# First attention of a decoder trunk: q and k copies in a used ring slot, keys turned between two v units, probabilities scaled by a diagonal while they are turned

## The reference, cut to what matters

```python
h = rms_norm(x, norm_mix[0])
p = h @ w_in_ab                        # columns: z (512) | q (768) | k (768) | v (768)
a_out = gmlp_spatial_gating(z)         # u * (w @ rms_norm(v) + b), causal, chunks of 128
q, k = rope(rms_norm(q)), rope(rms_norm(k))        # 12 heads of 64
for g in range(3):                                 # window/dilation groups, 4 heads each
    sc = q @ k.T / 8 ; masked by causality, window and dilation of the group
    m, l, o = max(sc), sum(exp(sc - m)), exp(sc - m) @ v / l
b_out = sum over g of softmax_g(m + log l) * o     # the groups merged by their denominators
x = x + concat(a_out, b_out) @ w_out_ab
x = x + swiglu(rms_norm(x, norm_ffn[0]), ffn weights)
# layer 2: MoBA attention and a short convolution, then top-2-of-8 SwiGLU experts
```

## Time and profile before

| | us |
|---|---|
| time, median of 3 runs | 1371.06 |
| the 3 runs | 1370.25, 1371.33, 1371.06 |
| the profiled execution, its own time | 1370.74 |
| its span in the profile | 1369.0 |
| TensorE busy | 1354.6 (99%) |
| VectorE busy | 1178.0 (86%) |
| ScalarE busy | 1017.7 (74%) |
| GpSimd busy | 121.3 (9%) |

### The profile page before, as it was taken

The page is one execution under the profiler, slowest core; times in us unless marked ns, Lnnn a source line. Parts: engine busy times, 40 slices in busy tenths (PEclk is TensorE's granted clock), DMA queues, the critical chain, the costliest instruction groups (busy, mean ns, idle before and its releaser), DMA issues.

```text
span 1369.0 us, 19886 instructions
## 1 busy us (share of the span) xinstructions
PE 1354.6 (99%) x6885; PEld 1140.2 (83%) x6885; DVE 1178.0 (86%) x1371; ACT 1017.7 (74%) x1189; POOL 121.3 (9%) x130
## 2 busy tenths in 40 slices
PE   9999999999999999999999999999999999999998
PEld 7778999988888788888888888888888888888886
DVE  5876655568969999999999999999999999999998
ACT  5656444456758778888888888888888888888886
POOL 1020000000230220200200110020020002003000
PEclk9999999999999999999999999999999999999999
DMA  9944543643657999999999999999999999999980
GB/s 346 362 139 170 185 154 124 217 153 123 247 202 294 364 381 359 393 397 372 368 394 397 353 391 400 369 370 394 396 352 392 398 360 378 394 386 361 393 335 31
DMA packets 184624, 430.90 MB, mean 315 GB/s; under 512 B 6076, under 2 KB 14032, under 8 KB 184576
## 3 DMA queue, kind: packets, MB, share of 16 engines
q1 hardware_dynamic: 181136, 422.81, 83.0%
q0 software_dynamic: 3440, 7.44, 2.5%
HBM read 425.68 MB, written 7.36 MB: 316 GB/s over the span
## 4 chain that ended last, share of the span: by engine, by line
PE 90%; DVE 6%; issue 1%; DMA 1%; ACT 1%; POOL 0%; DVEq 0%; POOLq 0%; ACTq 0%
PE psum L781 29%; PE psum L783 28%; PE psum L782 28%; DVE w_lo L428 2%; PE psum L1353 2%; DVE w_lo L410 1%; DMA slot_table<-routing,table_row 1%; DMA routing<-slot_table 0%; PE psum L813 0%; PE psum L1212 0%; PE psum L914 0%; POOL slot_table L705 0%; PE psum L1222 0%; DVE probs L2107 0%; PE psum L1055 0%
## 5 line engine op out<-in xcount | busy, mean ns | idle before, releaser
L428 DVE TENSOR_TENSOR w_lo<-raw_ring,w_hi 128x1024 fp32r<-128x1024 f32 x674 | 807.1, 1222 | 48.4 <-ACT w_hi L423 11.9
L423 ACT ACTIVATE w_hi<-raw_ring 128x1024 fp32r<-128x1024 f32 x675 | 713.1, 1061 | 165.4 <-PE psum L783 164.5
L781 PE MATMUL psum<-w_hi,xg_hi 128*128 128x512 f32 x896 | 351.1, 392 | 1.0 <-DVE w_lo L428 0.9
L783 PE MATMUL psum<-w_hi,xg_lo 128*128 128x512 f32 x896 | 348.9, 389 | 0.0
L782 PE MATMUL psum<-w_lo,xg_hi 128*128 128x512 f32 x896 | 348.7, 389 | 0.0
L410 DVE TENSOR_TENSOR w_lo<-raw_ring,w_hi 128x1024 fp32r<-128x1024 f32 x124 | 151.3, 1227 | 78.0 <-ACT w_hi L402 77.1
L402 ACT ACTIVATE w_hi<-raw_ring 128x1024 fp32r<-128x1024 f32 x124 | 130.0, 1058 | 93.9 <-PE psum L783 93.6
L781 PEld LDWEIGHTS psum<-w_hi,xg_hi 128*128 128x128 f32 x896 | 168.2, 188 | 35.9 <-issue 1.9
L783 PEld LDWEIGHTS psum<-w_hi,xg_lo 128*128 128x128 f32 x896 | 168.2, 188 | 35.3
L782 PEld LDWEIGHTS psum<-w_lo,xg_hi 128*128 128x128 f32 x896 | 168.3, 188 | 34.1
L781 PE MATMUL psum<-w_hi,moe_hT_hi 128*128 128x512 f32 x448 | 175.8, 392 | 0.5 <-DVE w_lo L428 0.5
(11 more groups left out here) (299 smaller groups left out, 1340.6 us busy)
## 6 DMA issues: line engine op xcount, KB each, us to landing
raw_ring<-in_moe_w_gate SPq DMA_DIRECT2D x56, 2048.0 KB, 10.7
raw_ring<-in_moe_w_up SPq DMA_DIRECT2D x56, 2048.0 KB, 10.9
raw_ring<-in_moe_w_down SPq DMA_DIRECT2D x56, 2048.0 KB, 10.5
raw_ring<-in_ffn_w_gate SPq DMA_DIRECT2D x5, 2048.0 KB, 8.0
raw_ring<-in_ffn_w_up SPq DMA_DIRECT2D x5, 2048.0 KB, 9.1
raw_ring<-in_ffn_w_down SPq DMA_DIRECT2D x5, 2048.0 KB, 10.3
raw_ring<-in_w_in_ab SPq DMA_DIRECT2D x4, 2048.0 KB, 19.6
raw_ring<-in_w_in_cd SPq DMA_DIRECT2D x4, 2048.0 KB, 8.2
```

Of the source, the lines that this page charges most:

```text
L423: act.activation(wh[:, v % SPLITS, :], moe_raw(i, q), ACT.Copy).then_inc(hi_ready, 1)
L428: dve.tensor_tensor(wl[:, v % SPLITS, :], moe_raw(i, q), wh[:, v % SPLITS, :].bitcast(F32), ALU.subtract).then_inc(lo_ready, 1)
L781: pe.matmul(out_, sh, mh_, start=start, stop=False)
L783: return pe.matmul(out_, sl, mh_, start=False, stop=stop)
```

## The change

- `qT` and `kT` move from `R0` (on `act_hi`) to the ring slot of the fifth tile (`A_SLOT` is 4), whose last unit is 19. Copies no longer wait for the last projection unit, but for `lo_ready` 20. SyncE's load of tile 11 into that slot gets a second wait, `s_done` 8.
- TensorE turns the keys after unit 20 and before unit 21, no longer after unit 21. ScalarE now copies five groups (0 to 4), VectorE one (5). ScalarE's table load for `Exp` follows the copies. The copy of v's last columns is shared: token tile 0 by ScalarE, token tile 1 by VectorE.
- The scalings of `probs[n]` are gone from VectorE and GpSimd. VectorE writes for each item a 128x128 diagonal of the inverse sums (`diag`, identity times a column), and `turn(n)` is an ordinary float32 matrix product of a block of `probs[n]` with this diagonal in place of a transposition with the identity. For items 0 to 3 the inversion is one instruction on four columns.
- VectorE's order changes: `maximum(4)` follows `cat_ab`, `cat_T` comes before `maximum(6)`, and the inverses are spread. The waits for `s_done` 8 in `cat_T` and `out_hi` are gone.

```diff
-        qT = at("qT", [6, SEQ], F32, R0)
-        kT = at("kT", [6, SEQ], F32, R0 + 6144)
+        A_SLOT = (first["out_ab_tile"] - 2) % RING
+        qT = at("qT", [6, SEQ], F32, base + A_SLOT * TILE * 4)
+        kT = at("kT", [6, SEQ], F32, base + A_SLOT * TILE * 4 + 6144)
+        diag = at("inverse_diagonals", [8, P], F32, R0 + 4096)
...
                 if t >= RING:
                     sp.wait_ge(lo_ready, tile_last[t - RING] + 1)
+                if t == RING + A_SLOT:
+                    sp.wait_ge(s_done, 8)
...
                 def turn(n):
-                    if n in P_POOL:
-                        pe.wait_ge(p_scaled_pool, P_POOL.index(n) + 1)
-                    else:
-                        pe.wait_ge(p_scaled, P_DVE.index(n) + 1)
+                    pe.wait_ge(p_inverse, n + 1)
...
-                        mm = pe.transpose(ps[:, bk, (b % 4) * P:(b % 4 + 1) * P], probs[n][:, b * P:(b + 1) * P], ident)
+                        mm = pe.matmul(ps[:, bk, (b % 4) * P:(b % 4 + 1) * P], probs[n][:, b * P:(b + 1) * P], diag[:, n, :],
+                                       start=True, stop=True)
...
-                pe.wait_ge(qkT_act, 3)
-                pe.wait_ge(qkT_dve, 3)
+                pe.wait_ge(qkT_act, 5)
+                pe.wait_ge(qkT_dve, 1)
                 scores_pair(0)
                 pe.wait_ge(proj_act, 6)
+                pe.wait_ge(v_last, 1)
                 scores_pair(1)
...
-            project(U_V4L, first["out_ab"], 0, 5)
+            project(U_V4L, U_V4L + 1, 0, 5)
             heads_T(3, 6)
+            project(U_V4L + 1, first["out_ab"], 0, 5)
...
+                act.wait_ge(lo_ready, U_V4L)
+                for i in range(3):
+                    turned_heads(i)
                 split_hi(act, first["out_ab"] + 2)
+                turned_heads(3)
                 act.wait_ge(gv_ms, 1)
                 act.activation(small[:, HSD:HSD + 8], small[:, HMS:HMS + 8], ACT.Sqrt).then_inc(gv_std, 1)
+                turned_heads(4)
                 act.preload_act_table(ACT.Exp)
...
+                def inverse(n0, n1):
+                    c = slice(3 * n0, 3 * n1 - 2, 3)
+                    dve.wait_ge(p_ready, n1)
+                    link(dve.reciprocal(small[:, RL:RL + 24][:, c], small[:, LS:LS + 24][:, c]))
+                    for n in range(n0, n1):
+                        dve.tensor_scalar(diag[:, n, :], ident, small[:, RL + 3 * n:RL + 3 * n + 1], None,
+                                          ALU.mult).then_inc(p_inverse, 1)
```

More of the change, by code:

```diff
@@ L146, in weight_stream @@
     first["out_ab"] = len(units)
+    first["out_ab_tile"] = len(tiles)
     units += by_rows(tile(w_out_ab, 0, 4, 0, D))
@@ L508, in decoder_trunk @@
         U_GV, U_V3, U_V4L = 12, 16, 20
+        QK_AB = 5
         QUARTER_BANKS = (5, 3, 4, 1)
@@ L656, in _ @@
             rope_tables(B_MQ, B_MK)
[L657 to L661, removed]
             for m in range(4):
@@ L1013, in c_scores_pair @@
                 if p == 0:
[L1014 removed]
+                    pe.wait_ge(qkT_act, QK_AB + 5)
                 else:
@@ L1563, in project_ab, with turned_heads @@
                 split_hi(act, first["out_ab"] + 1)
+                act.wait_ge(lo_ready, U_V4L)
+                for i in range(3):
+                    turned_heads(i)
                 split_hi(act, first["out_ab"] + 2)
+                turned_heads(3)
                 act.wait_ge(gv_ms, 1)
                 act.activation(small[:, HSD:HSD + 8], small[:, HMS:HMS + 8], ACT.Sqrt).then_inc(gv_std, 1)
+                turned_heads(4)
                 act.preload_act_table(ACT.Exp)
-            def heads_T():
                 act.wait_ge(unit_used, first["out_ab"])
[L1572 to L1577, removed]
-                split_hi(act, first["out_ab"] + 3)
+                act.activation(pv[:, 0, 512:QW], ps[:, 2, 0:QW - 512], ACT.Copy, scale=small[:, RS:RS + 1]).then_inc(proj_act, 1)
+                split_hi(act, first["out_ab"] + 3)
+            def turned_heads(i):
+                which, b0 = heads_order[i]
+                act.wait_ge(qkT_done, i + 1)
+                act.activation((qT, kT)[which][:, 2 * b0:2 * b0 + 2, :],
+                               ps[:, heads_banks[i], :].rearrange("p (b f) -> p b f", b=2), ACT.Copy).then_inc(qkT_act, 1)
             def project_cd(u0, u1):
@@ L2046, in project_ab @@
                                   ALU.mult, ALU.add).then_inc(gv_ms, 1)
+                which, b0 = heads_order[5]
+                dve.wait_ge(qkT_done, 6)
+                dve.tensor_copy((qT, kT)[which][:, 2 * b0:2 * b0 + 2, :],
+                                ps[:, heads_banks[5], :].rearrange("p (b f) -> p b f", b=2)).then_inc(qkT_dve, 1)
                 dve.wait_ge(gv_std, 1)
                 dve.reciprocal(small[:, HRS:HRS + 8], small[:, HSD:HSD + 8]).then_inc(gv_rstd, 1)
+                dve.wait_ge(unit_used, first["out_ab"])
+                dve.tensor_scalar(pv[:, 1, 512:QW], ps[:, 3, 0:QW - 512], small[:, RS + 1:RS + 2], None, ALU.mult).then_inc(v_last, 1)
             def c_project():
@@ L2085, in c_project @@
                         split_lo(dve, u + w + SPLITS)
-            def heads_T():
-                dve.wait_ge(unit_used, first["out_ab"])
-                for i in (1, 2, 5):
-                    which, b0 = heads_order[i]
-                    dve.wait_ge(qkT_done, i + 1)
-                    dve.tensor_copy((qT, kT)[which][:, 2 * b0:2 * b0 + 2, :],
-                                    ps[:, heads_banks[i], :].rearrange("p (b f) -> p b f", b=2)).then_inc(qkT_dve, 1)
             def attention():
@@ L2112, in maximum @@
                                       -1.0, None, ALU.mult).then_inc(max_ready, 1)
-                def inverse(n):
-                    c = 3 * n
-                    dve.wait_ge(p_ready, n + 1)
-                    ins = dve.reciprocal(small[:, RL + c:RL + c + 1], small[:, LS + c:LS + c + 1])
-                    if n in P_POOL:
-                        ins.then_inc(p_recip, 1)
-                    else:
-                        link(ins)
-                def scale(n):
-                    inverse(n)
-                    keys = 3 * P * (heads_of[n][0] + 1)
-                    dve.tensor_scalar(probs[n][:, 0:keys], probs[n][:, 0:keys], small[:, RL + 3 * n:RL + 3 * n + 1], None,
-                                      ALU.mult).then_inc(p_scaled, 1)
+                def inverse(n0, n1):
[5 more added lines that the diff above has]
+                                          ALU.mult).then_inc(p_inverse, 1)
                 def out_lo(t):
@@ L2139, in attention @@
                     maximum(n)
-                scale(0)
-                scale(1)
-                inverse(2)
-                inverse(3)
-                maximum(4)
+                inverse(0, 4)
                 dve.wait_ge(gy_done, 1)
@@ L2152, in attention @@
                 ins.then_inc(gcat_ready, 1)
+                maximum(4)
                 maximum(5)
-                scale(4)
-                inverse(5)
                 split_lo(dve, first["out_ab"])
+                inverse(4, 5)
+                cat_T()
                 maximum(6)
+                inverse(5, 6)
                 maximum(7)
-                cat_T()
                 split_lo(dve, first["out_ab"] + 1)
-                scale(6)
+                inverse(6, 7)
                 out_lo(0)
-                scale(7)
+                inverse(7, 8)
                 split_lo(dve, first["out_ab"] + 2)
```

14 lines of the change are left out of this document (4 added, 10 removed).

## The result

The changed kernel takes 1373.34 us, median of 22 runs (1372.24 to 1373.85), against 1370.99 for the kernel before (22 runs, 1370.02 to 1371.79). The ratio is 1.0017, 95% interval 1.0012 to 1.0023: 2.35 us slower. That is inside the 0.2% that the prediction called no change, but the interval is clear of 1, so the change does cost time; and it is close to the predicted 1373.1. The profiled span is 1371.3 us (1369.0 before).

What follows compares the result with a forecast made beforehand. TensorE, 90% of the chain, was taken to bound the kernel. +4.6 us for passes, -1.05 for the earlier start and holes shrinking by some 1.4 gave +2.2, forecast 1373.1 us, range 1370.5 to 1375.7.

Steps and rivals of the forecast that it cites:

- Part 1: Keys turned a unit earlier: first scores at 78.97 instead of 80.02, a gain of 1.05 us that nothing eats.
- Part 2: Scalings replaced by diagonals on VectorE: costed at nothing, with up to 0.5 us on the slow side in the range.
- thin covers: VectorE before TensorE: item 5's maximum covered by 0.2 us, its diagonal 93.1 for 93.49, last maximum 94.1 for 94.9.
- Part 3: Turns as float32 products: two passes a block at 0.1175 us each, 4.6 us more on TensorE over eight turns.
- the short turn: A turn of three blocks on TensorE: 0.70 us as products, 0.35 before with its start.
- The dense turns: Turns 6 and 7, in a stretch without holes: each 0.81 us longer.
- the total of +2.2: End of the output projection, and so the FFN's begin: 2.2 us later than before.
- The load of tile 11: SyncE's load now waits for the last scores, some 89.7; nearly 30 us of cover, cost nothing.
- Exposed weight loads: Rival at the eight turns: loads not hidden, 0.15 to 0.188 a pass, +4.2 to +6.9 us; chance 0.13.
- passes at 0.064: Nearly-free rival at the turns: a pass costs 0.06 as in the score rows, -0.1 to -0.25 us; chance 0.08.
- 4× faster for FP32: Skill's rule for transposing, taken as a rival: a product block costs four transpositions, 0.43, +8.7 us; chance 0.03.
- All holes go: Faster rival: freed engines remove all 3.1 us of TensorE's holes, passes hide there, 1367 to 1368; 0.06 including unseen causes.

Runs made afterwards that it cites:

- experiment 1: Changed kernel with the scalings on VectorE and GpSimd and transposed turns put back, keeping slot, early keys and v's shared copy: 1369.72 us, 0.9991 of the kernel before.
- experiment 3: Changed kernel with blocks turned by identity transposition, diagonals still made and waited for, division by the sum left out: 1370.78 us, 0.9998 of the kernel before.
- experiment 5: Changed kernel with the load of tile 11 held back until the last output pair of the attention: 1373.11 us.
- Experiment 8: As experiment 7, but GpSimd makes the four diagonals, inverses precede item 4's maximum, cat_T precedes the last maximum: 1368.72 us, 0.9983 of the kernel before.
- experiment 7: As experiment 6, but only items 0 to 3 divided behind the output product, items 4 to 7 beforehand: 1369.79 us, 0.9988 of the kernel before.
- experiments 2: Kernel before with the changed kernel's diagonals, float32 product turns and VectorE order, old key order and q/k copies: 1374.31 us, 1.0025 of the kernel before.
- 6: Changed slot and key order, probabilities transposed undivided, division behind the output product by spread diagonals: 1369.83 us, 0.9991 of the kernel before.

## Why the prediction was right, step by step

The measured times are given less 0.05, since the first query turns stand that much later than before.

| step | predicted | measured |
|---|---|---|
| first scores | 78.97 | 79.06 |
| scores of items 4 and 5 | 82.82 | 82.94 |
| turn 0 | 84.32 | 84.44 |
| first output pair | 86.55 | 86.88 |
| turn 3 | 87.36 | 87.68 |
| last scores | 88.08 | 88.55 |
| turn 4 | 90.97 | 91.44 |
| turn 5 | 93.49 | 94.03 |
| first output half | 94.92 | 95.37 |
| first FFN product | 113.5 | 113.71 |

- **Part 1** held: the copies are done long before, no hole eats the gain, and it arrives whole in experiment 1. It is 0.96 and not 1.05. The sum had left out two changes of product: the first product of unit 21 behind the key blocks takes 0.20 to the next one instead of 0.12, and from the last one to the first scores lie 0.21 instead of 0.12. The key blocks took 1.23 where it had 1.3.
- **Part 2**, nothing for VectorE's new work, held in its result. The thin covers were real: experiment 3 shows that a TensorE as fast as before would have waited for it at two new places.
- **Part 3** was right in its mechanism, twice the passes with the loads hidden, and near in the pass: 0.1175 taken, 0.112 measured in a run of them. What was mis-sized is the short turn: the path had 0.75 for turn 2 and 0.72 for turn 3, and from start to start they took 0.84 and 0.87. The row for it was there: the prediction put a transposed turn of three at 0.35, but turn 2 took 0.45 before, from 86.59 to 87.04. The chain of waits of the changed kernel (start, length, engine, line, count) shows them:

```profile
84.56 1.53 PE psum L928 x12
86.09 0.00 issue
86.09 0.91 PE psum L928 x6
87.00 0.81 PE psum L943 x12
87.81 0.86 PE psum L928 x6
```

  Turns 0 and 1 go in one run, 12 passes in 1.53; turns 2 and 3 stand alone, six passes in 0.91 and 0.86 (pieces of the chain run from the end of the one before). The first product of a turn lasts up to 0.377 where the median is 0.275, and a turn alone pays that, and the change to the product behind it, over six passes only. That is 0.24 of the 0.45 us by which the first output half comes later than predicted. Of the rest, 0.12 was there when turn 0 began, another 0.12 had come by the start of turn 2, which still waits for ScalarE's copy of turn 0 (the copy ends at 85.95, turn 2 starts at 86.09, 0.27 behind the last pass of turn 1), and 0.07 came from the round trip to turn 5; turn 5 itself gave 0.09 back (1.34 for 1.43).
- **The dense turns** gave some of it back: 1.36 and 1.26 for turns 6 and 7 against 0.63 and 0.58 before, 1.41 together where 1.62 was summed. So the total of +2.2 came out at +2.41 by two errors of opposite sign, +0.45 and -0.21; that it is so close is in part luck. The prediction's sum by terms shows the same. It had the turns at +4.6 and the holes behind the first scores, 2.25 in all, shrinking by 1.4. By the brackets they shrank by 0.98 (0.34 and 0.61 closed, 0.31 became 0.28), which leaves about +4.3 for the turns.
- **The load of tile 11** cost nothing, as said, and experiment 5 bears it out.
- **The rivals.** Exposed weight loads and passes at 0.064 fell with the 0.112. A block costs 0.22 as a product and about 0.105 turned by transposition, a ratio of 2.1. The Trainium skill, "TensorE: Matmul & The Clock Gate", section Terms, gives "4× faster for FP32" for the transpose mode without saying than what. Taken as four times as fast as an ordinary float32 product, the trace of the changed kernel does not agree. "All holes go" named the right free room but the wrong means: with twice the passes they were filled with the extra passes. Experiment 8 uses it for 1.6 us.

## What to carry to other kernels

Before work moves onto the engine that bounds the kernel, count in which holes it falls: eight passes in a hole cost nothing, and the same eight in a dense stretch 0.79 us. A change in two parts is worth taking apart: here one half gained 0.9 us and hid behind the other's 3.4. And when one queue is found late (experiment 7), look first for an instruction in it that is longer than its like (a group's mean hides it), and then at what stands ahead of the late instruction that an idle engine could do, even at nearly three times the duration.

## What was not expected of the hardware

- A change from one kind of product to another cost TensorE about 0.1 us beyond the passes, so 0.2 for a turn that stands alone: 0.377 for the first product of a turn against 0.275, and 0.21 against 0.112 from the last pass of turn 3 (88.39, its row's end less 0.28) to the last scores at 88.60. Why was not tested.
- Four `TENSOR_SCALAR` that write 128x128 diagonals took 0.87 or 0.88 us on VectorE in the changed kernel and in experiments 2, 3 and 6, with GpSimd idle, but 1.44 in experiment 7, where GpSimd scaled a block from 88.85 on, the same microsecond. All of the difference is in one of the four (0.847). The two behind it also ran beside the scaling and kept their length, and in the kernel before so did `w_lo` (1.21 us from 90.13, a scaling from 90.31). So VectorE is not slowed for as long as GpSimd works; that GpSimd held up this one instruction is a guess from one execution, and no run separates it. GpSimd's row in experiment 7:

```profile
88.85 2.31 POOL L670 TENSOR_SCALAR probs<-probs,small 128x768 f32<-128x768 f32 x1 [7.12 <-DVE small L2162]
```
